# A hybrid encoder layer: folding small work of the mixing stage into weights and tables, with its waits rearranged

## The reference

```python
h = rms_norm(x, g_mix);  z = h @ w_in                       # x: (2048, 1024)
c_val, c_gate, s_in = z[:, :512], z[:, 512:1024], z[:, 1024:]
u = c_val * sigmoid(c_gate)
y = causal_depthwise_conv31(u, conv_w) + conv_b
y_conv = silu(layer_norm(y, conv_ln_g, conv_ln_b))
y = s5_scan(s_in) + ssm_d * s_in                            # 32 groups of 16 channels, 64 states
y = gelu(y);  y_ssm = y * sigmoid(y @ glu_w + glu_b)
y_cat = concat(rms_norm(y_conv, g_branch[:512]), rms_norm(y_ssm, g_branch[512:]))
x = x + y_cat @ w_out
h = rms_norm(x, g_ffn)
x = x + hierarchical_moe(h)          # top group of 4, top 2 of its 8 experts, gated MLPs
out = rms_norm(x, g_final)
```

## Time and profile before

| | |
|---|---|
| median of three runs | 2018.83 us (2012.39 to 2023.08) |
| the profiled execution | 2024.83 us, of which its span 2023.3 |
| busy: PE, VectorE, ScalarE, GpSimd | 1705.8, 1126.5, 813.4, 574.4 us |
| mean granted TensorE clock | 0.900 of full speed |

### The profile page before, as it was taken

How to read it: one execution, slowest core, us unless ns; L and a number is a source line. 1 busy time by engine, 2 the same in 40 slices (tenths; PEclk the granted TensorE clock), 3 DMA queues, 4 the chain that set the end, 5 groups by cost and what they waited for, 6 DMA issues and landing times. The chain is left out here.

```text
span 2023.3 us, 33770 instructions
## 1 busy us (share of the span) xinstructions
PE 1705.8 (84%) x11301; PEld 1547.9 (77%) x11302; DVE 1126.5 (56%) x1855; ACT 813.4 (40%) x1063; POOL 574.4 (28%) x883
## 2 busy tenths in 40 slices
PE   6999996977475599999963999999999999999980
PEld 6999996955364478777753999988998888988970
DVE  6323212543364477777743664664566788666655
ACT  4222210223111234333221664664555777555553
POOL 0476773000243211454523121121211211121220
PEclk9999997578687699898876999999999999999995
DMA  7422115443995333332234887886688999888858
GB/s 217 130 95 94 71 65 119 91 132 118 264 311 145 92 115 112 108 95 94 92 152 165 268 287 236 282 283 229 209 278 301 307 376 374 264 271 276 280 164 342
DMA packets 179951, 399.74 MB, mean 198 GB/s; under 512 B 82063, under 2 KB 118929, under 8 KB 152752
## 3 DMA queue, kind: packets, MB, share of 16 engines
q1 hardware_dynamic: 154112, 332.17, 47.1%
q0 software_dynamic: 20080, 58.34, 11.9%
q10 hardware_dynamic: 5696, 8.39, 1.6%
HBM read 309.72 MB, written 89.13 MB: 197 GB/s over the span
## 5 line engine op out<-in xcount | busy, mean ns | idle before, releaser
L1681 DVE TENSOR_TENSOR expert_lo<-expert_raw,expert_hi 128x2048 fp32r<-128x2048 f32 x192 | 430.6, 2285 | 47.2 <-ACT expert_hi L1677 47.0
L1677 ACT CAST expert_hi<-expert_raw 128x2048 fp32r<-128x2048 f32 x192 | 361.8, 1911 | 17.6 <-DMA expert_raw<-in_experts 9.5
L554 PE MATMUL proj_p_z<-proj_h_hi,proj_w_hi 128*128 128x256 f32 x768 | 219.7, 286 | 9.6 <-DVE proj_u_out L495 7.7
L555 PE MATMUL proj_p_z<-proj_h_lo,proj_w_hi 128*128 128x256 f32 x768 | 217.8, 284 | 0.0
L556 PE MATMUL proj_p_z<-proj_h_hi,proj_w_lo 128*128 128x256 f32 x768 | 217.7, 283 | 0.0
L2081 PE MATMUL moe_p_g0u<-expert_hi,moe_xh 128*128 128x256 f32 x736 | 210.2, 286 | 1.5 <-DVE moe_xl L1994 1.5
L2082 PE MATMUL moe_p_g0u<-expert_hi,moe_xl 128*128 128x256 f32 x736 | 205.9, 280 | 0.0
L2083 PE MATMUL moe_p_g0u<-expert_lo,moe_xh 128*128 128x256 f32 x736 | 205.8, 280 | 0.0
L2096 PE MATMUL moe_p_y<-expert_hi,moe_hh 128*128 128x512 f32 x368 | 153.2, 416 | 13.0 <-DVE moe_hl L2005 13.0
L554 PEld LDWEIGHTS proj_p_z<-proj_h_hi,proj_w_hi 128*128 128x128 f32 x768 | 147.8, 193 | 11.2 <-issue 11.2
L1923 POOL DMA_INDIRECT residual<-moe_y,moe_ids_s x46 | 78.5, 1708 | 259.5 <-ACT moe_y L1950 252.5
(11 more groups left out here) (432 smaller groups left out, 4239.6 us busy)
## 6 DMA issues: line engine op xcount, KB each, us to landing
expert_raw<-in_experts SPq DMA_DIRECT2D x192, 1024.0 KB, 7.8
ffn_input<-mix_h SPq DMA_DIRECT2D x17, 512.0 KB, 4.0
proj_x_sb<-in_x SPq DMA_DIRECT2D x8, 1024.0 KB, 5.6
mix_x_sb<-in_x SPq DMA_DIRECT2D x16, 512.0 KB, 5.5
residual<-mix_x SPq DMA_DIRECT2D x16, 512.0 KB, 2.7
out<-final_x SPq DMA_DIRECT2D x16, 512.0 KB, 5.9
proj_w_raw<-in_w_in SPq DMA_DIRECT2D x8, 768.0 KB, 7.5
final_x<-residual SPq DMA_DIRECT2D x3, 2048.0 KB, 16.4
```

The lines of the kernel that those rows point to most:

```text
L554: nc.tensor.matmul(o, whi, h_hi[:, half, c], start=c == 0 if start is None else start, stop=False)
L555: nc.tensor.matmul(o, whi, h_lo[:, half, c], start=False, stop=False)
L1677: self.nc.scalar.copy(self.hi[:, u], self.raw[:, u]).then_inc(self.hi_done, 1)
L1681: tensor_tensor(self.lo[:, u], self.raw[:, u], self.hi[:, u].bitcast(FP32), ALU.subtract).then_inc(self.lo_done, 1)
```

## The change

- The reciprocal root starts from half its argument, so that it needs eleven operations instead of twelve, and eight where the argument is one column (`rsqrt_column`).
- The skip term isn't computed in the mixing stage any more: `ssm_d` is put on the diagonal of the lag-0 block of each group's chunk kernel. GpSimd does that in `convolution_and_tables`, and SP's store of each unit waits for it. The loads of `s_in` go.
- `g_branch` is multiplied into the output weights in `ssm`: a small load ahead of the pieces of `w_out`, a scaled copy on ScalarE, a three-operand operation on VectorE. VectorE and ScalarE wait at the stage's start until `glu_in` has reached 32, that is for this load and for the first load of gating weights.
- In `mix`, rounding and remainder of a branch become one 1024-wide operation each instead of four 256-wide ones. The statistics of the norm are combined with a hardware aggregation; VectorE computes scale and shift, and ScalarE normalises (`center`).
- The parameters are packed on the host: three columns in one load (`cols_in`), three further loads (`params`), issued after the first rows of x. The waits stand where a parameter is first used; ScalarE's wait for pads and slot table stands ahead of its first square of x.

The diff, cut to its core:

```diff
-RSQRT_STEPS = 12
-def rsqrt(nc, step, y, a, t, u):
-    yi, ai = y.bitcast(INT32), a.bitcast(INT32)
-    step(nc.vector.tensor_scalar(yi, ai, 1, None, ALU.logical_shift_right))
-    step(nc.vector.tensor_scalar(yi, yi, -1.0, float(0x5F3759DF), ALU.mult, ALU.add))
-    step(nc.vector.tensor_scalar(a, a, -0.5, None, ALU.mult))
+RSQRT_STEPS = 11
+RSQRT_COLUMN_STEPS = 8
+def rsqrt_seed(nc, step, y, half):
+    yi, hi = y.bitcast(INT32), half.bitcast(INT32)
+    step(nc.vector.tensor_scalar(yi, hi, 1, None, ALU.logical_shift_right))
+    step(nc.vector.tensor_scalar(yi, yi, -1.0, float(0x5F3759DF - 0x400000 - 2 ** 31), ALU.mult, ALU.add))
+def rsqrt(nc, step, y, half, t):
+    rsqrt_seed(nc, step, y, half)
     for _ in range(3):
         step(nc.vector.tensor_tensor(t, y, y, ALU.mult))
-        step(nc.vector.tensor_tensor(u, t, a, ALU.mult))
-        step(nc.vector.scalar_tensor_tensor(out=y, in0=u, scalar=1.5, in1=y, op0=ALU.add, op1=ALU.mult))
+        step(nc.vector.tensor_tensor(t, t, half, ALU.mult))
+        step(nc.vector.scalar_tensor_tensor(out=y, in0=t, scalar=-1.5, in1=y, op0=ALU.add, op1=ALU.mult))
+def rsqrt_column(nc, step, y, half, t):
+    rsqrt_seed(nc, step, y, half)
+    for _ in range(3):
+        step(nc.vector.tensor_scalar(t, y, y, half, ALU.mult, ALU.mult))
+        step(nc.vector.scalar_tensor_tensor(out=y, in0=t, scalar=-1.5, in1=y, op0=ALU.add, op1=ALU.mult))
...
+        d_cols, d_diag = sb("d_cols", [GC, GRP]), sb("d_diag", [GC, GRP, GC])
...
+            pool.wait_ge(b_in, 32)
+            nc.gpsimd.tensor_tensor(d_diag[:, :, :], ident[0:GC, 0:GC].unsqueeze(1).broadcast_to([GC, GRP, GC]),
+                                    d_cols[:, :].unsqueeze(2).broadcast_to([GC, GRP, GC]), ALU.mult).then_inc(kern_ready, 1)
+            pool.wait_ge(kern_ready, 1)
+            with pool.Fori(0, NU) as n:
+                lag0 = kern[:, :, (T8 - 1) * GC:T8 * GC]
+                pool.wait_ge(tab_copied, 3 * n + 2)
+                nc.gpsimd.tensor_tensor(lag0, lag0, d_diag[:, :, :].rearrange("p (u g) c -> p u g c", g=UG)[:, bass.ds(n, 1)].squeeze(1),
+                                        ALU.add).then_inc(kern_ready, 1)
...
+            sp.dma_start(d_cols[:, :], ssm_d).then_inc(b_in, 16)
...
+                sp.wait_ge(kern_ready, n + 2)
...
+        def gain_of(i, half, k):
+            return branch_gain[:, bass.ds(i * 4 + (2 * half + k // 2), 1)]
...
+            sp.dma_start(branch_gain[:, :], g_branch).then_inc(glu_in, 16)
...
+            dve.wait_ge(glu_in, 32)
...
-                        V.tensor_tensor(piece(weights["wo_lo"], i, half, k), wo_raw[:, k],
-                                        piece(weights["wo_hi"], i, half, k).bitcast(FP32), ALU.subtract).then_inc(wo_lo_done, 1)
+                        V.scalar_tensor_tensor(out=piece(weights["wo_lo"], i, half, k), in0=wo_raw[:, k], scalar=gain_of(i, half, k),
+                                               in1=piece(weights["wo_hi"], i, half, k).bitcast(FP32),
+                                               op0=ALU.mult, op1=ALU.subtract).then_inc(wo_lo_done, 1)
...
+            act.wait_ge(glu_in, 32)
...
-                            nc.scalar.copy(piece(weights["wo_hi"], i, half, k), wo_raw[:, k]).then_inc(wo_hi_done, 1)
-                        act.wait_ge(glu_in, n * 16 + 16)
+                            nc.scalar.activation(piece(weights["wo_hi"], i, half, k), wo_raw[:, k], ACT.Copy,
+                                                 scale=gain_of(i, half, k)).then_inc(wo_hi_done, 1)
+                        act.wait_ge(glu_in, n * 16 + 32)
...
-            vectors = ((LNG, ln_g), (LNB, ln_b), (DD, ssm_d), (GLB, glu_b), (GBC, g_branch[0:CW]), (GBS, g_branch[CW:D]))
             def load_front(n):
                 sp.dma_start(conv_in[:, :, :], tiles("conv")[n]).then_inc(conv_ld, 16)
             def load_ssm(n):
                 sp.dma_start(y_in[:, :, :], tiles("y")[n]).then_inc(y_ld, 16)
-                sp.dma_start(s_in[:, :, :], tiles("s")[n]).then_inc(s_ld, 16)
             load_front(0)
             load_ssm(0)
-            for to, v in vectors:
-                load_column(nc, sp, cols[:, to], v).then_inc(params, 16)
-            sp.dma_start(gain[:, :], g_ffn.partition_broadcast(P)).then_inc(params, 16)
-            sp.dma_start(wr[:, :, 0:NG], w_rg.rearrange("(c p) n -> p c n", p=P)).then_inc(params, 16)
-            sp.dma_start(wr[:, :, NG:NL], w_re.rearrange("(c p) n -> p c n", p=P)).then_inc(params, 16)
-            sp.dma_start(br[:, 0:NG], b_rg.partition_broadcast(P)).then_inc(params, 16)
-            sp.dma_start(br[:, NG:NL], b_re.partition_broadcast(P)).then_inc(params, 16)
+            sp.dma_start(cols[:, :, :], columns).then_inc(cols_in, 16)
             for t in range(2):
                 sp.dma_start(x_sb[:, t], x_rows[0][t]).then_inc(x_ld[t], 16)
+            sp.dma_start(gain[:, :], g_ffn.partition_broadcast(P)).then_inc(params, 16)
+            sp.dma_start(wr[:, :, :], w_router).then_inc(params, 16)
+            sp.dma_start(br[:, :], b_router.partition_broadcast(P)).then_inc(params, 16)
...
-                pool.wait_ge(v_done, n + 1)
+                pool.wait_ge(y_ld, 16 * (n + 1))
...
-            act.wait_ge(pads, 32)
-            act.wait_ge(table_st, 32)
-            act.wait_ge(params, 16 * PARAMS)
-            act.wait_ge(halved, 1)
...
+            def center(n):
+                act.wait_ge(ln_scale, n + 2)
+                for t, bank in enumerate((pa, pb)):
+                    last = nc.scalar.activation(yn[:, t], bank[:, :], ACT.Identity, scale=rs[:, t:t + 1], bias=shift[:, t:t + 1])
+                last.then_inc(yn_done, 1)
...
-                for c in range(CT):
-                    last = nc.scalar.activation(cat_hi[:, par, c], yc[:, c], ACT.Copy, scale=cols[:, GBC, c:c + 1])
-                last.then_inc(c_hi_done, 1)
+                nc.scalar.copy(cat_hi[:, par, 0:CT], yc[:, :, :]).then_inc(c_hi_done, 1)
...
+                if q == 0:
+                    act.wait_ge(pads, 32)
+                    act.wait_ge(table_st, 32)
...
+                    center(n)
...
-            dve.wait_ge(params, 16 * PARAMS)
-            V.tensor_scalar(half_glb[:, :], cols[:, GLB, :], 0.5, None, ALU.mult).then_inc(halved, 1)
-            F1 = 7 + RSQRT_STEPS
-            FO = 1 + RSQRT_STEPS
+            dve.wait_ge(cols_in, 16)
+            V.tensor_scalar(half_glb[:, :], cols[:, GLB, :], 0.5, None, ALU.mult).then_inc(ln_scale, 1)
+            F1 = 2 + RSQRT_STEPS
+            FO = 1 + RSQRT_COLUMN_STEPS
...
-            def skip(n):
-                dve.wait_ge(y_ld, 16 * (n + 1))
-                dve.wait_ge(s_ld, 16 * (n + 1))
-                for c in range(CT):
-                    last = V.scalar_tensor_tensor(out=y_in[:, c], in0=s_in[:, c], scalar=cols[:, DD, c:c + 1],
-                                                  in1=y_in[:, c], op0=ALU.mult, op1=ALU.add)
-                last.then_inc(v_done, 1)
...
-                dve.wait_ge(stats_done, n * 2 + 2)
-                me, mo, ve, vo = (bn[:, :, i] for i in (1, 4, 2, 5))
-                mean, dif, var = mv[:, :, 0], mv[:, :, 1], mv[:, :, 2]
-                step(V.tensor_tensor(mean, me, mo, ALU.add))
-                step(V.tensor_tensor(dif, me, mo, ALU.subtract))
-                step(V.tensor_tensor(var, ve, vo, ALU.add))
-                step(V.tensor_scalar(mean, mean, 0.5, None, ALU.mult))
-                step(V.tensor_tensor(dif, dif, dif, ALU.mult))
-                step(V.scalar_tensor_tensor(out=var, in0=dif, scalar=CW / 4.0, in1=var, op0=ALU.mult, op1=ALU.add))
-                step(V.tensor_scalar(squares[:, 0, 0:2], var, 1.0 / CW, EPS, ALU.mult, ALU.add))
+                dve.wait_ge(stats_done, n * 3 + 2)
+                for t in range(2):
+                    step(V.bn_aggr(mv[:, t], bn[:, t]))
+                V.tensor_scalar(squares[:, 0, 0:2], mv[:, :, 1], 0.5, 0.5 * EPS, ALU.mult, ALU.add).then_inc(stats_done, 1)
+                dve.wait_ge(stats_done, n * 3 + 3)
                 w = 2
                 if not first(n):
                     read_sums(n - 1)
                     w = 6
-                rsqrt(nc, step, rs[:, 0:w], squares[:, 0, 0:w], squares[:, 1, 0:w], squares[:, 2, 0:w])
-                for t, bank in enumerate((pa, pb)):
-                    last = V.tensor_scalar(yn[:, t], bank[:, :], mv[:, t, 0:1], rs[:, t:t + 1], ALU.subtract, ALU.mult)
-                last.then_inc(yn_done, 1)
+                rsqrt(nc, step, rs[:, 0:w], squares[:, 0, 0:w], squares[:, 1, 0:w])
+                V.scalar_tensor_tensor(out=shift[:, :], in0=mv[:, :, 0], scalar=-1.0, in1=rs[:, 0:2],
+                                       op0=ALU.mult, op1=ALU.mult).then_inc(ln_scale, 1)
...
-                for c in range(CT):
-                    last = V.scalar_tensor_tensor(out=cat_lo[:, par, c], in0=yc[:, c], scalar=cols[:, GBC, c:c + 1],
```

(15 more changed lines are left out.)

86 lines of the change are left out of this document (45 added, 41 removed).

## The result

The changed kernel takes 1991.47 us (median of four runs, 1987.62 to 1995.24) against 2020.95 us for the kernel before on the same chip: ratio 0.986, 95% interval 0.983 to 0.989. Run again on a second chip with more rounds it took 1991.63 us, ratio 0.987 (0.985 to 0.989). Forecast were 1998 us, 1986 to 2008, and faster with 0.85: the sign and the range held, the gain was larger than forecast, 29.5 us between the two profiled executions instead of 20.9.

What follows compares the result with a forecast made beforehand. PE was taken to set the mixing stage's pace. Terms of -29.6 (mixing), +8.5 and +1.0 (state-space) and -0.8 (end) sum to -20.9, turning the median 2018.8 into 1997.9, stated as 1998 us; range 1986 to 2008.

Steps and rivals of the forecast that it cites:

- The new wait in the state-space stage: State-space stage start: waiting for gating weights delays VectorE's first product by 10.4 us; third block absorbs 1.9, leaving +8.5.
- The rival that called it free: State-space stage: gating weights land with the turn tables, or third block's slack is larger; 1989 us, chance 0.12.
- paid again at each load: Rival, state-space stage: loads of blocks three and four each add 10.4 us; 2020.6, chance 0.03 fully, 0.12 half.
- Start (a): Mixing stage start: earlier squares, shorter norm chain and merged rounding bring the first output product 13.7 us earlier.
- The rule on the port: Mixing stage: by the skill's rule a 1024-wide split holds GpSimd's sums back 1.2 us; start gain 12.5 instead of 13.7.
- Term (d): Mixing stage, two steps after a choice with another step behind them: 4.0 us less each, -8.0 together.
- Centring: Mixing stage norm: the two normalising passes move from VectorE to ScalarE, estimated at 1.4 us for both.
- Second step (b): Mixing stage, second step: the gating product's 2.08 us wait goes, -2.1.
- (c) to (e): Mixing steps: four short logit waits -2.5, two steps after a choice -8.0, step after the last choice -2.5.
- the clock comes back: Rival, mixing stage: fewer waits keep PE at 2.4 GHz, up to 3.4 us per step change; down to 1974, chance 0.07.
- Last tile (f): Mixing stage, last tile's norm: four small operations fewer with PE waiting behind it, -0.8 us.
- GpSimd's diagonal: Kernel tables before their store: GpSimd's adds of the direct term are hidden, taken as 0; uncovered up to 1.9 us.

Runs made afterwards that it cites:

- delay runs: Changed kernel with two or four unused VectorE products added behind each of the three expert choices: 2004.95 us (ratio 0.992) and 2020.11 us (ratio 0.998).

## Why the prediction was right, and where it was short

- **The new wait in the state-space stage**: +10.4 forecast for the first product, 9.85 by absolute time and 10.6 from the stage's own start measured; removing it gave 10.5 back. It is the one loss in the change. The rival that called it free is out, and it was not paid again at each load. But the stage's sum is right by luck: it grew 9.1 instead of 9.5, and the 1.9 us that the third block was to absorb were not absorbed there. The wait is 10.5 and the scaled operations are 2.1 instead of 1.0, together 12.6; 3.5 came back elsewhere. Of that, 2.8 came back between the third block's first and third product (12.0 us instead of 14.8), and as much in the run without the wait (11.9); why is open.
- **Start (a)**: -13.7 forecast, -14.0 measured. Its steps, each counted from the last state-space product: squares -10.8 (forecast -11.1), gating product -12.9 (-13.1). Behind that the sum is right for the wrong reasons. Rounding gave its 0.6, the port took 1.05 back (2.30 us for GpSimd's add), and the clock gave some 1.5: 2.8 us at half speed after the first gating product, where it had been 5.8.
- **The rule on the port** of the Trainium skill ("SBUF — State Buffer", Who interferes with whom) was weighed and not used. The row of the changed kernel agrees with it: 2.33 us for an add of 1.26 beside one merged subtraction. Four narrow operations let GpSimd in between and pay themselves, 3.24 and 6.96 us. Both sides of the trade come to one: merging costs GpSimd 1.05 us and saves VectorE 2 to 5.7. Term (d) missed a part of it: behind a choice it put the second split at 2.5 us, as if it had to let GpSimd's add go first, and it took 1.26.
- **Centring**: 0.78 us a pass, as estimated from the rows (0.4 to 1.05, taken 0.7) and nearer still to the 0.80 estimated from the Trainium skill ("ScalarE: Activation LUTs", What ACT_TABLE_LOAD costs). "ScalarE has the time" held; undone, the start was 1.8 us longer.
- **Second step (b)**: -2.1 forecast; first output to second gating product 16.9 before, 13.6 changed, -3.3.
- **The terms that were too small are (c) to (e)**, with the place right and the size wrong. The waits went as said: 9.2 us of waits for logits became 0.3 (1.4 in the second profile). In a step behind a choice PE's idle time fell from 4.9 to 1.5 us, 3.4 and so within the 4.0 of the forecast. But "PE can use no more than its wait" is not a bound: half clock fell from 13.7 us, of which 2.2 had been idle, to 6.8, and this gave another 2.4. Together they are the 5.8 us by which each of these steps became shorter (6.1 and 7.4 in the second profile) instead of 4.0. All after (b) gave 21.8 instead of 13.8. The delay runs show it from the other side: 1.2 to 1.6 us for each us. The rival "the clock comes back" had this mechanism and up to 3.4 us a step; it got 0.07, as an all-or-nothing case. It came in part: half-clock stretches went behind the choices and stayed once a step.
- **Last tile (f)**: -0.8 forecast and not seen. From the last output product to the first load of expert weights it is 14.3 us before, 13.9 and 16.1 in the two profiles of the changed kernel.
- **Centring and the clock**: the changed kernel pays up to 3.4 us in each step for a stretch that was mostly gone in the runs with a filler of 0.6 us, another order, or the old centring. In the time that was 4 to 7 us of the median, not the 9 to 16 of the profiled stages. Nothing in the forecast priced what the edits do to this stretch.
- **GpSimd's diagonal** at nothing: no cost seen. **Final norm**: -0.8 forecast; from its first load to the end 46.2 us instead of 47.1.

## What to carry to other kernels

When TensorE sets the pace, price a removed wait at more than its length if half-clock stretches stand near it, and read the granted clock per step before and after: two steps with the same products may differ by 3 us, and two executions of one kernel may differ in which steps these are. Compare the mean clock of all runs before a profile is called typical. Then look at the thinnest work of the step (small products and idleness in a row) and put wide products into or between it; the two runs that did had a ratio of 0.981 instead of 0.986 and 0.987. When a wait is taken away, ask what the engine that is now free will run beside: GpSimd's cubes, no longer held by the skip term, doubled the time of the narrow splits in the run that had both. A parameter that is loaded for a later use should ride on a wait that is already there: sharing a semaphore with a large load cost this kernel's state-space stage 10 us.

## What the hardware showed that I had not expected

- The clock of TensorE fell behind 0.77 us of idleness with logits, transposes and sums, and not behind the same row of work in another kernel, nor in another step of one kernel (40.9 and 37.3 us); with three products of 0.6 us together in the idleness the half-clock time went from 42 to 52 us down to 21. What decides in between is open.
- Four 256-wide operations of VectorE took 6.96 us beside GpSimd's 1024-wide ones and 3.24 beside its 512-wide add, one 1024-wide operation 1.23 us.
- One and the same kernel's experts' stage took 887.5 and 891.9 us, and 885.6 to 895.6 over all profiles; why is open.
